# A gated hybrid decoder block on eight Trainium2 cores: identity products for turning rows replaced by transposing DMAs, and the planner's ranks by TensorE time

## The reference

```python
h = rms_norm(x, norm1_g)
cols = h @ w_in                       # 4864 columns: q, f, i, g of the recurrence, q, k, v of the attention, two gates
# recurrence, 4 heads of 128x128 state:  S_t = diag(f_t) S_{t-1} + k_t v_t^T,  o_t = S_t^T q_t
o_a = rms_norm(o, out_g) * silu(g)
# sliding window of 128, 8 query and 2 key heads of 64, ALiBi, a sink logit in the denominator
o_b = swa_sink_attention(q, k, v, q_g, k_g, sinks)
mixed = sigmoid(gate_a) * (o_a @ w_branch_a) + sigmoid(gate_b) * (o_b @ w_branch_b)
x = x + mixed @ w_out
u = rms_norm(x, norm2_g) @ w_up       # 2 x 2816 columns: gate, val
x = x + (gelu(causal_conv3(gate)) * val) @ w_down
```

## Time and profile before

| | us |
|---|---|
| median of 3 runs | 3765.95 |
| the runs | 3761.4, 3765.95, 4421.3 |
| the profiled execution, own time | 3760.1 |
| its span on the slowest core | 3758.6 |
| spans of the eight cores | 3747.6 to 3758.6 |
| granted TensorE clock of the cores, mean | 0.991 to 0.994 |

### The profile page before, as it was taken

How to read it: one execution, slowest core, us unless ns; L and a number is a source line. 1 busy time by engine, 2 the same in 40 slices (tenths; PEclk the granted TensorE clock), 3 DMA queues, 4 the chain that set the end, 5 groups by cost and what they waited for, 6 DMA issues and landing times.

```text
span 3758.6 us, 64664 instructions; the slowest of 8 cores (3747.6 to 3758.6 us)
## 1 busy us (share of the span) xinstructions
PE 3604.0 (96%) x21154; PEld 1968.3 (52%) x21516; DVE 2046.0 (54%) x3275; ACT 2128.2 (57%) x3595; POOL 520.6 (14%) x1176
## 2 busy tenths in 40 slices
PE   5779999999999999999999999999999999999999
PEld 2334645546455464654646455464554646456466
DVE  4355455564555646556565555645556465555544
ACT  5567374664746647365483745747375483755722
POOL 1203112010120201102011020201202011020100
PEclk9899999999999999999999999999999999999999
DMA  8879969847465564655646465474655646566464
GB/s 188 180 225 201 258 180 243 257 157 249 143 227 189 181 228 153 222 177 194 225 157 228 161 227 194 159 251 157 205 188 192 230 156 215 178 203 212 136 227 147
DMA packets 205814, 742.35 MB, mean 198 GB/s; under 512 B 22832, under 2 KB 23216, under 8 KB 205488
## 3 DMA queue, kind: packets, MB, share of 16 engines
q1 hardware_dynamic: 191088, 687.95, 54.3%
q0 software_dynamic: 13536, 48.24, 8.2%
q10 hardware_dynamic: 864, 2.00, 0.2%
HBM read 687.76 MB, written 98.57 MB: 209 GB/s over the span
## 4 chain that ended last, share of the span: by engine, by line
PE 86%; ACT 6%; issue 3%; DMA 3%; DVE 1%; POOL 0%; ACTq 0%; another core or an unknown queue 0%; DVEq 0%; SPq 0%; POOLq 0%
PE bank L652 86%; ACT fa L608 2%; DMA wF<-wscr 1%; ACT ef L608 1%; ACT L608 1%; ACT xs L609 1%; DMA wA<-wscr 1%; DMA gB<-c_g 0%; ACT ba L608 0%; DVE fa L630 0%; DMA wF<-wall 0%; DVE ef L625 0%; DMA wA<-wall 0%; PE bank L660 0%; ACT hT L608 0%
## 5 line engine op out<-in xcount | busy, mean ns | idle before, releaser
L652 PE MATMUL bank<-h2T,wF 128*128 128x512 bf16 x5520 | 1282.0, 379 | 40.1 <-ACT ef L608 22.7
L652 PE MATMUL bank<-hT,wA 128*128 128x512 bf16 x4069 | 963.1, 381 | 24.8 <-DMA wA<-wscr 8.4
L652 PEld LDWEIGHTS bank<-h2T,wF 128*128 128x128 bf16 x5632 | 537.0, 98 | 692.4 <-issue 81.3
L625 DVE SCALAR_TENSOR_TENSOR ef<-bank,cft,ef 128x512 f32<-128x512 f32 x704 | 520.7, 747 | 311.8 <-ACT ef L608 265.4
L652 PEld LDWEIGHTS bank<-hT,wA 128*128 128x128 bf16 x4224 | 408.6, 98 | 473.1 <-issue 28.7
L652 PE MATMUL bank<-wF,act 128*128 128x256 bf16 x5632 | 648.9, 273 | 4.2 <-DMA wF<-wscr 4.2
L652 PEld LDWEIGHTS bank<-wF,act 128*128 128x128 bf16 x5632 | 549.1, 98 | 104.0 <-issue 5.5
L608 ACT ACTIVATE ef<-bank,cft 128x512 f32<-128x512 f32 x352 | 273.4, 777 | 327.3 <-PE bank L652 264.4
L630 DVE TENSOR_TENSOR act<-ef,bank 128x512 bf16<-128x512 f32 x352 | 241.5, 686 | 360.4 <-PE bank L652 351.1
L608 ACT ACTIVATE ef<-ef 128x512 f32<-128x512 f32 x352 | 215.4, 627 | 207.4 <-DVE ef L625 205.5
L608 ACT ACT_TABLE_LOAD x235 | 301.5, 1283 | 47.3 <-PE bank L652 31.7
(11 more groups left out here) (87 smaller groups left out, 3358.0 us busy)
## 6 DMA issues: line engine op xcount, KB each, us to landing
wF<-wscr SPq DMA_DIRECT2D x430, 512.0 KB, 4.6
wA<-wscr SPq DMA_DIRECT2D x396, 512.0 KB, 4.9
xt<-x SPq DMA_DIRECT2D x128, 512.0 KB, 7.6
x1scr<-xt SPq DMA_DIRECT2D x64, 512.0 KB, 4.5
xt<-x1scr SPq DMA_DIRECT2D x64, 512.0 KB, 5.8
x<-x1scr SPq DMA_DIRECT2D x64, 512.0 KB, 8.2
y<-x SPq DMA_DIRECT2D x64, 512.0 KB, 6.0
wF<-wall POOLq DMA_DIRECT2D x50, 512.0 KB, 11.8
```

Source lines behind the costliest of these rows:

```text
L625: return P.record("dve", lambda h: h.scalar_tensor_tensor(out=res(out), in0=res(in0), scalar=scalar, in1=res(in1), op0=op0, op1=op1), read ...
L652: inst = h.matmul(res(out), lhsT=res(lhsT), rhs=res(rhs), start=st, stop=sp_)
```

## The change

1. `norm_block` keeps the identity products in path A for tiles 0 and 1 (`tA` = 1) and in path F for tile 0 (`tF` = 0). After these, eight transposing DMAs from SP, SBUF to SBUF, 128x128 bf16 (32 KB) each, write `xs` into `hT` or `h2T`.
2. `hg_block` keeps the key transposition by TensorE in tile 0 (`tK` = 0); after it four transposing DMAs per block write `kd` into `kt`. These depend on `kd` alone, no longer on `vtm[b]` and the last state update.
3. A new helper `DMAT` records such a group: one semaphore, all with the dependencies of the first, in order.
4. Ranks: with `pm` = 1.0 an operation's place in its path is the share of the path's TensorE cost recorded before it, not i/n.
5. `CAPS` pA from 6 to 5; `foff` from 0.2 to 0.3; the assumed cost of the attention's score products from T // 2 to T columns. The bound `dw` on the DMA backlog is set to 1e9 ns.

```diff
-CAPS = dict(pA=6, pF=5)
-TUNE = dict(nxt=4, nxs=4, nwa=5, nwf=5, dA=18, dF=10, dF2=99, rF=1, skew=4, gc=0, foff=0.2, hold=6000.0)
+CAPS = dict(pA=5, pF=5)
+TUNE = dict(tK=0, pm=1.0, tA=1, tF=0, dw=1e9, nxt=4, nxs=4, nwa=5, nwf=5, dA=18, dF=10, dF2=99, rF=1, skew=4, gc=0, foff=0.3, hold=6000.0)
...
+            tot = sum(o.cost for o in ops if o.eng == "pe") or 1.0
+            cum = 0.0
+            m = TUNE["pm"]
             for i, o in enumerate(ops):
-                o.prio = base + i / n
+                o.prio = base + (1.0 - m) * i / n + m * cum / tot
+                if o.eng == "pe":
+                    cum += o.cost
...
                 for o in ready[e]:
                     st = o.ready
+                    if o.nbytes and dma_free - TUNE["dw"] > st:
+                        st = dma_free - TUNE["dw"]
...
+        def DMAT(pairs, reads, dst, sem, nbytes):
+            mine = []
+            for out, in_ in pairs:
+                o_ = P.record("sp", lambda h, out=out, in_=in_: h.dma_start(out=res(out), in_=res(in_), transpose=True), reads, [dst], 450.0, 2000.0, SET_ANY, sem, nbytes)
+                if mine:
+                    o_.deps.difference_update(mine)
+                    o_.deps.update(mine[0].deps)
+                    o_.order.add(mine[-1])
+                mine.append(o_)
+
+        hsem = [[P.new_sem() for b in range(NB)] for i in range(2)]
...
-            for half in range(2):
-                bk = bank(pool)
-                PE([(bk[:, c4 * 128:(c4 + 1) * 128], xs[:, (half * 4 + c4) * 128:(half * 4 + c4 + 1) * 128], ident, True, True, 128) for c4 in range(4)],
-                   [xs] + C("cbb"), [bk])
-                CP("act", hdst[:, half * 4:(half + 1) * 4, b * 128:(b + 1) * 128], bk.lz().rearrange("p (c t) -> p c t", t=128), [bk], [bhdst[b]], psum=True)
+            if ti <= (TUNE["tA"] if which == 0 else TUNE["tF"]):
+                for half in range(2):
+                    bk = bank(pool)
...
+                return
+            DMAT([(hdst[:, kc, b * 128:(b + 1) * 128], xs[:, kc * 128:(kc + 1) * 128]) for kc in range(8)], [xs], bhdst[b], hsem[which][b], 32768)
...
-                bkT = bank(pPA)
-                pv = bkT.lz().bitcast(BF16)
-                oT = TR([pv[:, h * 128:(h + 1) * 128] for h in range(4)], [kd[:, h, sl] for h in range(4)], bkd + C("cbb") + [bvtm[b]], [bkT])
-                after(oT, last_u[0])
+                kt = vb(pSM, "kt")
+                if ti <= TUNE["tK"]:
+                    bkT = bank(pPA)
...
+                    CP("act", kt.lz(), pv[:, 0:512].rearrange("p (h t) -> p h t", t=128), [bkT], [kt], psum=True)
+                else:
+                    DMAT([(kt[:, h, :], kd[:, h, sl]) for h in range(4)], bkd, kt, kt, 32768)
...
-                    PE([(bks[kv].lz().rearrange("p (g t) -> p g t", t=128), kn[hs[kv], b + kb, :], qn[hs[kv], :, sl], True, True, T // 2) for kv in range(2)],
+                    PE([(bks[kv].lz().rearrange("p (g t) -> p g t", t=128), kn[hs[kv], b + kb, :], qn[hs[kv], :, sl], True, True, T) for kv in range(2)],
```

More of the change, by code:

```diff
@@ L783, in bank, with norm_block @@
             return VBuf(pr[0], "ps", pr[1], pr[2])
-        def norm_block(which, b, xv, hdst, bhdst, pool):
+        def norm_block(ti, which, b, xv, hdst, bhdst, pool):
             st4 = nst[which]
@@ L792, in norm_block @@
             STT(xs.lz(), xv.lz(), st4[:, b, 2:3], gB[which][:], ALU.mult, ALU.mult, [xv, bn] + C(f"gB{which}"), [xs], n=D, psum=False)
-            for half in range(2):
-                bk = bank(pool)
-                PE([(bk[:, c4 * 128:(c4 + 1) * 128], xs[:, (half * 4 + c4) * 128:(half * 4 + c4 + 1) * 128], ident, True, True, 128) for c4 in range(4)],
-                   [xs] + C("cbb"), [bk])
-                CP("act", hdst[:, half * 4:(half + 1) * 4, b * 128:(b + 1) * 128], bk.lz().rearrange("p (c t) -> p c t", t=128), [bk], [bhdst[b]], psum=True)
+            if ti <= (TUNE["tA"] if which == 0 else TUNE["tF"]):
+                for half in range(2):
+                    bk = bank(pool)
+                    PE([(bk[:, c4 * 128:(c4 + 1) * 128], xs[:, (half * 4 + c4) * 128:(half * 4 + c4 + 1) * 128], ident, True, True, 128) for c4 in range(4)],
+                       [xs] + C("cbb"), [bk])
+                    CP("act", hdst[:, half * 4:(half + 1) * 4, b * 128:(b + 1) * 128], bk.lz().rearrange("p (c t) -> p c t", t=128), [bk], [bhdst[b]], psum=True)
+                return
+            DMAT([(hdst[:, kc, b * 128:(b + 1) * 128], xs[:, kc * 128:(kc + 1) * 128]) for kc in range(8)], [xs], bhdst[b], hsem[which][b], 32768)
         def fm(pool, w, c0, src, bsrc, ncol=128, stride=256):
@@ L906, in hg_block @@
                 after(oS, last_u[0])
-                bkT = bank(pPA)
-                pv = bkT.lz().bitcast(BF16)
-                oT = TR([pv[:, h * 128:(h + 1) * 128] for h in range(4)], [kd[:, h, sl] for h in range(4)], bkd + C("cbb") + [bvtm[b]], [bkT])
-                after(oT, last_u[0])
+                kt = vb(pSM, "kt")
+                if ti <= TUNE["tK"]:
+                    bkT = bank(pPA)
+                    pv = bkT.lz().bitcast(BF16)
+                    oT = TR([pv[:, h * 128:(h + 1) * 128] for h in range(4)], [kd[:, h, sl] for h in range(4)], bkd + C("cbb") + [bvtm[b]], [bkT])
+                    after(oT, last_u[0])
+                    CP("act", kt.lz(), pv[:, 0:512].rearrange("p (h t) -> p h t", t=128), [bkT], [kt], psum=True)
+                else:
+                    DMAT([(kt[:, h, :], kd[:, h, sl]) for h in range(4)], bkd, kt, kt, 32768)
                 sT = vb(pSM, "sT")
                 TT("dve", sT.lz(), bkS.lz().rearrange("p (h t) -> p h t", t=128), mask_st[:].rearrange("p (o t) -> p o t", o=1).broadcast_to([128, 4, 128]), ALU.mult, [bkS] + C("mask"), [sT], psum=True)
-                kt = vb(pSM, "kt")
-                CP("act", kt.lz(), pv[:, 0:512].rearrange("p (h t) -> p h t", t=128), [bkT], [kt], psum=True)
                 gb_ap = gdec[par][:, :, b:b + 1].broadcast_to([128, 4, 128])
@@ L1011, in stage_f @@
                 after(o_, lead.get(("F", ti - 1)))
-                norm_block(1, b, xv, h2T, bh2T, pPF)
+                norm_block(ti, 1, b, xv, h2T, bh2T, pPF)
             for c in range(NFC):
```

2 lines of the change are left out of this document (1 added, 1 removed).

## The result

The changed kernel takes 4376.9 us against 3762.7 us for the kernel before on the same chip: 1.163 times as long, 95% interval 1.160 to 1.166. I had said 3700 us and a range of 3640 to 3850. In some executions of any of these kernels the cores of one die or of both run at a lower granted clock and take longer, and these executions are left out of every time and ratio from here on; a time is the median of the others.

The account below looks back on a forecast made before the run. TensorE's instruction stream was taken as the bound. Removing 65.4 us and adding 0 turned the profiled 3760.1 us into 3694.7, and the runs' median 3765.95 into 3700.5, stated as 3700 us; range 3640 to 3850.

Parts of the forecast that it names:

- What bounds the kernel, and the products: TensorE's instruction stream bounds the steady part; 1168 identity products removed at 0.056 us each save 65.4 us.
- (a): SP's queue: 80 transposing issues a period, taken at 0.5 us each, hidden; room until 1.8 us each.
- (b): Latency to hT: 45.7 us of cover between the last normed block and the next tile's first reader; hidden.
- (c): Latency to h2T and of the keys: covers of 43.7 us and 35.6 us before TensorE's first read; hidden.
- (d): Time of the 16 DMA engines per transposition: bounds 0.10 and 1.08 us, estimate 0.3 us, costing nothing.
- Rival A: DMA engines become the bound in the 114 us rush; at 0.85 us a transposition 200 us lost, 3966 us; chance 0.22.
- Order: New ranks, later path F, five PSUM banks for path A, full-length score products: zero, ends -30 and +60 us.

Follow-up runs that it names:

- plan-only run: The changed kernel with all transpositions left on TensorE and the rest of the change kept: 3797.1 us, ratio 1.009 to the kernel before.

## Why the prediction was wrong

**What bounds the kernel, and the products.** Right in size: 65.4 us were counted for 1168 products; 62.8 were measured. That they come through whole isn't shown. From the plan-only run to the one with one DMA per block, 48 us of them reach the time.

**(a) Issue time.** This is the step that failed: "No row shows a transposing issue; until it takes 145/80 = 1.8 us SP still has room. I take 0.5 us, hidden." The value and the test are both wrong. The issue holds SP 1.232 us, two and a half times my value, and my nearest row, a burst of three plain issues at 0.63 each, was of another form. The test averaged SP's room over a period. On that average there still is room: SP waits 1327.7 us for TensorE in the changed kernel, from 2411.9. But the sixteen transpositions between 2538 and 2562 us don't use the room of the whole period, they use the room ahead of the next weight piece, in a stretch where a piece of wF lasts TensorE 32 products. I did the sum for the engines over the 114 us rush (36.5 us free for 64) and not for the queue: 64 x 1.23 = 79 us of SP, beside the issues of some 50 other transfers, strictly in order. With those at 0.32 us to 0.52 us each (the single weight pieces among the transpositions) that is 95 to 105 us of 114, before any wait of SP's own. That sum would have shown how tight it is.

I also missed whose number it was. The kernel's order is made by a planner which assumed 0.45 us; where an assumed cost is off by 0.8 us and sixteen stand on end, the plan is 12 us late by the last. Correcting the number alone gave back 443 of 614 us.

**(b), (c) Latency.** The covers held where SP was not in arrears; TensorE waited for a transposed tile itself only twice in the changed kernel, once 25.6 us for h2T and once 20.8 us for kt. What I left out is that a transposition issued late makes other DMAs late, x1scr and its reload, and through them VectorE's act.

**(d) Engine time.** Right: 0.21 us by the runs, between the bounds 0.10 and 1.08, my value 0.3; a plain copy of the same tile takes 0.20. Rival A had the right place (the rush) and the right victims (wF pieces) with the wrong resource: the engines' share there fell to 0.53 where I had asked for 0.95. Its price, 200 us, was a third of the true one.

Of the two pages of the Trainium skill that I weighed, the trace decides for both in a way that I hadn't considered. "VectorE: DVE Perf Modes", section "The three transpose paths", has 1309 ns for a block: near the 1232 ns for which the issuing queue is held, but that isn't time of the DMA engines. "Advanced Engine Details and Errata", section "X-Bar Transpose (TRN2)", has the transfers about as fast as plain ones: by the engines that is so, 0.21 us against 0.20 for a plain copy of the same 32 KB.

**Order.** I took 0, with -30 and +60 as ends. Alone it is +35 us (1.007 to 1.012), and with the small transpositions 34 us (4376.9 against 4342.5). With one DMA per block the sixth bank is worth 19 us by the medians, 25 by the ratios; the sign of the rest changes from version to version, as the runs with the old plan and with the keys in one DMA show.

**Clock.** No step of mine had it: I multiplied at 2.4 GHz throughout. Once TensorE stands still 6 to 10 us at a time, part of the rest runs at the lower level, and the same products took at least 95 us more, a sixth of the loss. No run separates the clock from the gaps.

## What to carry to other kernels

Ask of an added DMA not only what the engines spend on it, but for how long it holds the queue that issues it, and add that up over the stretch in which the next urgent transfer stands behind it, not over the whole period. Where the hold goes by the instruction, issue few large ones: eight blocks in one instruction, planned at its measured hold, turned a loss of 16% into no change, and with a PSUM bank given back into a gain of 0.9%. Where a planner writes the order, a new kind of operation needs its measured cost before its order can be trusted.

## What the runs showed of the hardware that I had not expected

A transposing DMA from SP holds SP 1.23 us in the median for 128x128 in bf16, and for 128x1024 1.23 us at the least and 1.27 and 1.70 us in the median; a plain copy of 32 KB from SBUF to SBUF holds it 0.60 us, though single loads of 512 KB from DRAM hold it 0.32 us. By the queue's packets a 128x128 transposition makes 160: (377968 - 191088) / 1168, with 191088 for the same queue before. A plain copy of the tile makes 144, and takes the engines as long.
